# No meeting of the engines between gates and mixing, nor between attention and up projections, with single waits in its place

## Chip, cores and metric

The kernel runs on one core of a Trainium2 chip. TensorE (PE) multiplies, VectorE (DVE), ScalarE (ACT) and GpSimd (POOL) do the rest, SyncE (SP) starts the loads of weights, POOL those of most other tensors. The engines run side by side and order themselves by semaphores alone. The metric is the time of one execution on the device in microseconds (us), given as the median of several runs.

## What is computed

Two transformer blocks on 512 positions, width 2048. The change touches the first one only, where the input projection, three attentions, a gated sum of three up projections and an output projection follow each other:

```python
(a_q, a_ckv, i_q, i_k, i_w, a_gate, b_q, b_k, b_v, b_gate,
 c_q, c_gate, mix_gate) = split_cols(h @ w_in[l], IN_SIZES)
...
oa = dsa_attention(qa, ka, va, iq, ik, iw, bias_a, topk) * jax.nn.silu(a_gate)
...
ob = sliding_window_attention(qb, kb, vb, sinks_b[l], bias_b) * jax.nn.silu(b_gate)
...
oc = memory_attention(qc, kc, vc) * jax.nn.silu(c_gate)
g_a, g_b, g_c = jnp.split(jax.nn.sigmoid(mix_gate + gate_bias[l]), N_BRANCH, axis=-1)
merged = g_a * (oa @ w_up_a[l]) + g_b * (ob @ w_up_b[l]) + g_c * (oc @ w_up_c[l])
x = x + merged @ w_o[l]
```

`dsa_attention` picks each query's keys by an indexer: `score = sum over 16 heads of iw * relu(iq @ ik)`, then the 128 highest.

## The kernel before

**Chunks and groups.** All weights are cut into chunks of 128 x 2048 numbers (1 MB). A projection group `g` yields 256 columns for 512 positions from two chunks, 2g and 2g+1, of 48 products each. A product of full precision is three matmuls (`mm3`, L391 to L393), since every chunk is split into a rounded part and the rest: ACT writes `w_hi` (`split_hi`, L375) and DVE `w_lo` (`split_lo`, L380). There are two buffers each of `w_raw`, `w_hi` and `w_lo`, even chunks in the first, odd ones in the second. PE may not start a chunk before both parts are there (`chunk_ready`), and ACT may not overwrite `w_hi` before PE is done with the chunk two before (`chunk_used`). A chunk's 48 matmuls are 8 row tiles x 2 column halves x 3. SP loads `w_raw` as soon as DVE is through with it.

**Stages.** First come the query groups and 8 gate groups (`G_GATE`), whose two halves lie in PSUM banks 0, 1 or 2, 3 in turn; ACT takes Tanh (L1266), DVE multiplies (L1763) and POOL stores to `g_d` (L2249). Then 24 mixing groups from `G_MIX` on fill banks 0 and 1; ACT takes their Tanh (L1285, `mix_out`) and POOL stores them to `mix_d`. In the first 8 of them `idx_units` (L764) puts 12 small indexer matmuls, in banks 2 to 7, ahead of a group's four quarters (`gemm_part`); ACT takes Relu of these (L1298), DVE adds them up. In the other 16, attention items 2 to 17 stand between the quarters: logits in banks 2 and 3, transposed probabilities in 4 and 5, the result in bank 6; DVE writes it out as `o_st` (L1948, semaphore `o_ready`), POOL stores it to `o_d`.

**Up projections.** Eight groups from `G_UP` on (`up_group`). Their moving operand is the attention result: POOL loads `o_d` in six parts of 3, 3, 4, 4, 1 and 1 row tiles into `o_raw` (L2328, `PARTS_1`), ACT rounds each part into `act_b[0]` (L1106, `part_hi`) and DVE writes the rest into `act_b[1]` (L1956, `part_lo`). `act_b` lies where the attention's operands lay. A group holds three sums: row tiles 0 to 5 in banks 0, 1; 6 to 9 in banks 2, 3; 10 to 15 in banks 4, 5. DVE multiplies each with the gates in `mixg` (L1967), which POOL loads from `mix_d` (L2350), and adds them (L1980, L1985).

**Meetings.** Between the gates and the mixing, and again between the attention and the up projections, all four engines call `meet`: each lets its own work end (`drain`), counts up the semaphore `barrier` and waits until all four have done so. For the second meeting POOL counts up early, while its last stores are still to come. Nothing that an engine has behind the meeting starts before the last one arrives.

Of the kernel before, what the change touches and what calls it, by code (L numbers as in the profile page):

```python
# [22 lines left out]
ALU = mybir.AluOpType  # L23
# [103 lines left out]
def build_kernel(nc, wst, xt_in, mem_in, par_in, con_in, pos_in, tab1_in, tab2_in, rpb_in, lng_in, lnb_in, out):  # L127
# [21 lines left out]
    with ctx:  # L149
# [213 lines left out]

        def meet(eng, n):

            eng.drain().then_inc(barrier, 1)
            eng.wait_ge(barrier, 4 * n)

# [190 lines left out]
        def _(pe):  # L559
# [185 lines left out]
            meet(pe, 1)  # L745


# [19 lines left out]
            with pe.Fori(0, 4) as i:  # L767
                for par in range(2):
                    g, t = 2 * i + (G_MIX + par), 2 * i + par
                    for hs in range(4):  # L770
                        if hs == 0:
                            pe.wait_ge(iq_loaded[par], 16 * i + 16)
                            idx_units(t, par)
                            pe.wait_ge(ev_act, g - 1)
                        gemm_part(g, hs, act_a)
# [113 lines left out]

            up_group(0, first=True)  # L890
# [210 lines left out]
        def _(act):  # L1101
# [173 lines left out]
            meet(act, 1)  # L1275
# [62 lines left out]
            for kind, it0, n in (("B", 2, ITEMS_B), ("C", 8, ITEMS_C), ("A", 12, ITEMS_A)):  # L1338
                with act.Fori(0, n // 2) as i:
                    for par in range(2):  # L1340
                        it = 2 * i + (it0 + par)
                        g = 2 * i + (G_MIX + 6 + it0 + par)
                        for hs in range(4):
                            att_act(kind, it, hs)
                            if hs == 0:
                                split_hi(act, 2 * g + 1, 1)
                            elif hs == 2:
                                split_hi(act, 2 * g + 2, 0)
                        mix_out(g, i, par, 6 + it0)
            meet(act, 2)  # L1350

# [6 lines left out]
            for p in range(len(PARTS_1)):  # L1358
                part_hi(PARTS_1, p, 1)
            with act.Fori(0, 8) as j:  # L1360
                g = j + G_UP
                hi2(g)
                act.wait_ge(up_ch, 5 * j + 5)
                copy(act_a[0][:, bass.ds(2 * j, 2), :], m_acc[:], scale=0.5).then_inc(up_hi, 1)

# [121 lines left out]
        def _(dve):  # L1487
# [309 lines left out]
            meet(dve, 1)  # L1797
# [152 lines left out]
            meet(dve, 2)  # L1950
# [8 lines left out]
            for p in range(len(PARTS_1)):  # L1959
                part_lo(PARTS_1, p, 0)  # L1960
            with dve.Fori(0, 8) as j:
                g = j + G_UP

                def gated(c, dst):

                    for n in range(2):
                        last = dve.scalar_tensor_tensor(out=dst[:, n, :], in0=mixg[:, c, n, :], scalar=1.0,  # L1967
                                                        in1=bank[2 * c + n][:], op0=ALU.add, op1=ALU.mult)
                    last.then_inc(up_ev, 1)

                split_lo(dve, 2 * g + 1, 1)
# [18 lines left out]
                                         op0=ALU.mult, op1=ALU.subtract).then_inc(up_lo, 1)  # L1990

# [187 lines left out]
        def _(pool):  # L2179
# [70 lines left out]
            meet(pool, 1)  # L2250
# [57 lines left out]

            def step(n_it, i, par, g, nxt):

                mix_store(g, i, par, n_it)
                pool.wait_ge(o_ready, 2 * i + (n_it - 5 + par))
                pool.nop(nofuse=True)
                pool.dma_start(o_d[2 * i + (n_it - 8 + par)], o_st[par][:]).then_inc(o_out[par], 16)
# [15 lines left out]
            for n_it, count, same, after in ((8, ITEMS_B, next_b, load_c), (14, ITEMS_C, load_c, next_a),  # L2330
# [4 lines left out]
                if not after:  # L2335
                    pool.drain().then_inc(barrier, 1)

                    for s in range(2):
                        pool.wait_ge(o_out[s], 128)
                    for p in range(4):  # L2340
                        load_part(o_d, PARTS_1, p)
                i = count // 2 - 1
                for par in range(2):
                    step(n_it, i, par, 2 * i + (G_MIX + n_it + par), after)
            pool.wait_ge(o_out[0], 144)
            load_part(o_d, PARTS_1, 4)
            pool.wait_ge(barrier, 8)
# [8 lines left out]
            pool.wait_ge(o_out[1], 144)  # L2356
            load_part(o_d, PARTS_1, 5)
# [88 lines left out]
            pool.wait_ge(barrier, 12)  # L2446
# [81 lines left out]
```

## Time and profile before

| | |
|---|---|
| median of 3 runs | 2747.0 us (2746.95 to 2748.36) |
| the profiled execution: its time, its span | 2748.42 us, 2746.9 us |
| PE busy | 2651.1 us, 97% of the span |
| DVE, ACT, POOL busy | 1191.5, 765.5, 249.7 us |
| mean granted TensorE clock | 0.984 of full speed |
| PE on the chain that ended last | 92% |

The span runs from the first to the last instruction of the profiled execution. Times in rows count from its start. "Idle before" is the time in which an engine did nothing ahead of an instruction, with what released it. An engine's time is worth something only where PE waits for it. The granted clock says at what share of 2.4 GHz the matmuls of a stretch ran; 0.50 is the lower level, 1.2 GHz.

### The profile page before, as it was taken

Reading aid. Unit: us, or ns where it says so; the run is one execution under the profiler, and the core shown is the slowest. Engines: PE = TensorE matmul, PEld = TensorE weight load, DVE = VectorE, ACT = ScalarE, POOL = GpSimd, SP = SyncE. Lnnn points to the kernel's source line nnn. Section 1 sums busy time; section 2 is a strip of 40 time slices with the busy share of each in tenths; the row PEclk is TensorE's granted clock in tenths of the full one; section 3 lists DMA queues with packets and bytes.
Section 4 is the critical chain, followed back from the end, with each engine's and each line's share of the span. In section 5 each row is a group of like instructions: output and inputs, shape, how many; then the busy total and the mean of one; then the engine's idle time right before and its main releaser. Section 6 shows DMA issues by size and latency. Waiting matters only on the chain.

```text
span 2746.9 us, 34039 instructions
## 1 busy us (share of the span) xinstructions
PE 2651.1 (97%) x12748; PEld 2132.9 (78%) x12748; DVE 1191.5 (43%) x2113; ACT 765.5 (28%) x1092; POOL 249.7 (9%) x385
## 2 busy tenths in 40 slices
PE   6959999998999999999999999999999999999998
PEld 5758888887777778888788888777777777777787
DVE  4636222222335775545455332444444444434425
ACT  5321221222332332323222222332233223222321
POOL 4111000000000110111000000000001111211000
PEclk8989999999999999999999999999999999999999
DMA  7454433333343443435444444232232222323432
GB/s 219 114 163 153 143 107 115 115 122 110 111 141 114 148 139 123 161 138 194 151 162 159 158 148 135 90 98 94 94 107 87 92 89 93 99 99 105 180 117 93
DMA packets 70545, 348.80 MB, mean 127 GB/s; under 512 B 11699, under 2 KB 11699, under 8 KB 42275
## 3 DMA queue, kind: packets, MB, share of 16 engines
q1 hardware_dynamic: 38148, 241.28, 25.9%
q0 software_dynamic: 32320, 106.46, 12.2%
q8 instruction: 53, 0.87, 0.1%
q14 instruction: 24, 0.20, 0.0%
HBM read 298.74 MB, written 50.45 MB: 127 GB/s over the span
## 4 chain that ended last, share of the span: by engine, by line
PE 92%; DMA 2%; DVE 2%; ACT 1%; issue 1%; POOL 0%; POOLq 0%; SPq 0%; ACTq 0%; DVEq 0%
PE bank L391 25%; PE bank L393 25%; PE bank L392 25%; PE bank L1069 5%; PE bank L955 2%; PE bank L937 2%; PE bank L1093 2%; PE bank L925 1%; DMA w_raw<-wst 1%; DVE w_lo L380 1%; PE bank L824 1%; PE bank L805 1%; PE bank L786 1%; DMA mem_raw<-mem_t 1%; PE bank L764 1%
## 5 line engine op out<-in xcount | busy, mean ns | idle before, releaser
L380 DVE TENSOR_TENSOR w_lo<-w_raw,w_hi 128x2048 fp32r<-128x2048 f32 x211 | 486.9, 2308 | 527.8 <-ACT w_hi L375 527.8
L391 PE MATMUL bank<-act_a,w_hi 128*128 128x512 f32 (+1 forms) x1672 | 660.8, 395 | 5.5 <-ACT stage L1285 4.1
L393 PE MATMUL bank<-act_a,w_hi 128*128 128x512 f32 (+1 forms) x1672 | 652.5, 390 | 0.0
L392 PE MATMUL bank<-act_a,w_lo 128*128 128x512 f32 (+1 forms) x1672 | 651.8, 390 | 0.0
L391 PE MATMUL bank<-act_b,w_hi 128*128 128x512 f32 x1280 | 505.2, 395 | 7.7 <-DVE act_b L1956 5.2
L375 ACT ACTIVATE w_hi<-w_raw 128x2048 fp32r<-128x2048 f32 x210 | 401.0, 1910 | 395.9 <-PE bank L393 316.0
L393 PE MATMUL bank<-act_b,w_hi 128*128 128x512 f32 x1280 | 499.6, 390 | 0.0
L392 PE MATMUL bank<-act_b,w_lo 128*128 128x512 f32 x1280 | 499.2, 390 | 0.0
L391 PEld LDWEIGHTS bank<-act_a,w_hi 128*128 128x128 f32 (+1 forms) x1672 | 314.2, 188 | 79.9 <-issue 16.1
L393 PEld LDWEIGHTS bank<-act_a,w_hi 128*128 128x128 f32 (+1 forms) x1672 | 313.9, 188 | 66.8
L392 PEld LDWEIGHTS bank<-act_a,w_lo 128*128 128x128 f32 (+1 forms) x1672 | 314.5, 188 | 63.3
L391 PEld LDWEIGHTS bank<-act_b,w_hi 128*128 128x128 f32 x1280 | 240.9, 188 | 57.9 <-issue 7.3
L393 PEld LDWEIGHTS bank<-act_b,w_hi 128*128 128x128 f32 x1280 | 240.8, 188 | 50.9
L392 PEld LDWEIGHTS bank<-act_b,w_lo 128*128 128x128 f32 x1280 | 241.1, 188 | 48.3
L1380 ACT ACTIVATE prob<-prob,nmx 128x512 f32<-128x512 f32 (+1 forms) x128 | 77.8, 609 | 346.4 <-DVE nmx L1493 346.4
L1069 PE MATMUL bank<-w_hi,act_b 128*128 128x512 f32 x384 | 119.5, 393 | 0.4 <-ACT act_b L1106 0.4
L1285 ACT ACTIVATE stage<-bank,half_b 128x512 f32<-128x512 f32 x48 | 30.3, 683 | 231.0 <-PE bank L393 231.0
L2017 DVE CUSTOM_DVE_ANT_0 prob<-bank,b 128x512 f32<-128x512 f32 x64 | 41.7, 688 | 104.8 <-PE bank L925 104.7
L1493 DVE TENSOR_SCALAR prob<-prob,rden 128x256 f32<-128x256 f32 (+1 forms) x216 | 83.5, 396 | 6.8
L1069 PEld LDWEIGHTS bank<-w_hi,act_b 128*128 128x128 f32 x384 | 72.3, 189 | 15.6 <-issue 0.7
L1069 PE MATMUL bank<-w_lo,act_b 128*128 128x512 f32 x192 | 75.0, 391 | 0.0
L955 PEld LDWEIGHTS bank<-prob_t,v_tok 128*64 128x64 f32 x768 | 40.9, 137 | 38.6 <-issue 35.8
(286 smaller groups left out, 2205.7 us busy)
## 6 DMA issues: line engine op xcount, KB each, us to landing
w_raw<-wst SPq DMA_DIRECT2D x215, 1024.0 KB, 4.9
mix_d<-stage POOLq DMA_DIRECT2D x24, 512.0 KB, 3.0
mixg<-mix_d POOLq DMA_DIRECT2D x8, 1536.0 KB, 6.8
b<-rows_2d POOLq DMA_DIRECT2D x16, 448.0 KB, 7.4
x_raw<-x_t SPq DMA_DIRECT2D x8, 512.0 KB, 8.2
q_d<-stage POOLq DMA_DIRECT2D x8, 512.0 KB, 3.2
g_d<-stage POOLq DMA_DIRECT2D x8, 512.0 KB, 3.2
qb<-q_d POOLq DMA_DIRECT2D x16, 256.0 KB, 3.9
```

What stands on the lines that cost most here:

```text
L375: act.activation(w_hi[s][:], w_raw[s][:], ACT.Copy).then_inc(hi_ready, 1)
L380: dve.tensor_tensor(w_lo[s][:], w_raw[s][:], w_hi[s][:].bitcast(F32), ALU.subtract).then_inc(lo_ready, 1)
L391: pe.matmul(out_ap, l_hi, r_hi, start=start, stop=False)
L392: pe.matmul(out_ap, l_lo, r_hi, start=False, stop=False)
L393: return pe.matmul(out_ap, l_hi, r_lo, start=False, stop=stop)
L937: last = pe.transpose(bank[T_BANK[e]][:, b * P:(b + 1) * P], prob[:, 2 * (cc % 2) + e, b * P:(b + 1) * P], ident)
L955: last = pe.matmul(bank[O_BANK][64 * e:64 * e + 64, c * P:(c + 1) * P], v_tok[par][:, vb, 64 * e:64 * e + 64], prob_t[e][:, b, :], start=( ...
L1069: last = pe.matmul(bank[4 * s + b][:], act_b[l][:, k, b * P:(b + 1) * P], wt(r[c % 2], kt, 0, 2 * GC, 2 * GC), start=(k == 0 and n == 0 an ...
L1093: last = pe.matmul(dst[:], act_b[l][:, k, b * P:(b + 1) * P], wt(r[c], kt, 0, 2 * GC, 2 * GC), start=False, stop=(k == KT - 1 and n == 2), ...
L1380: act.activation(pr, pr, ACT.Exp, bias=nmx[:, cc, e:e + 1], accum_out=rs[:, cc, e:e + 1]).then_inc(e2_ready, 1)
L1493: return dve.tensor_scalar(dst, src, by, None, ALU.mult)
L2017: ins = dve.tensor_tensor_reduce(out=dst, in0=src[:], in1=b2[2 * par + e][:, 384 - P * tb:896 - P * tb], scale=1.0, scalar=-3.4e38, op0=AL ...
```

## The change

Both meetings and the function `meet` go, and single semaphores take their place.

At the first one PE starts the first mixing group's first quarter (banks 0, 1) as soon as the gate group before the last has been read from these banks, and puts the 12 indexer matmuls behind this quarter, with a wait for the last gate group's DVE read. Elsewhere the indexer stays ahead of the first quarter. Two of the 8 items are now written out ahead of the loop.

At the second one the three sums of an up group are in banks 2, 3 (row tiles 0 to 5), 0, 1 (6 to 9) and 4, 5 (10 to 15), so that the first one does not touch the banks of the last mixing group; PE waits for `o_ready` 18 (the last item's result written), and for ACT's last Tanh only before the second sum. ACT rounds parts 0 and 1 ahead of the last Tanh, and the odd weight chunk ahead of parts 4 and 5; DVE keeps the same order. POOL stores the last item's result and loads parts 4 and 5 ahead of the last store to `mix_d`; the gates' load comes after that store, as before. The drains go too.

```diff
-            meet(pe, 1)
-
+            pe.wait_ge(ev_dve, G_MIX - 2)
...
-            with pe.Fori(0, 4) as i:
+            def idx_group(i, par):
+
+                g, t = 2 * i + (G_MIX + par), 2 * i + par
+                first = isinstance(i, int) and i == 0 and par == 0
+                if first:
+                    pe.wait_ge(ev_act, G_MIX - 2)
+                    gemm_part(g, 0, act_a)
+                    pe.wait_ge(ev_dve, G_MIX - 1)
+                    pe.wait_ge(qcp, 10)
+                pe.wait_ge(iq_loaded[par], 16 * i + 16)
+                idx_units(t, par)
+                pe.wait_ge(ev_act, g - 1)
+                for hs in range(1 if first else 0, 4):
+                    gemm_part(g, hs, act_a)
...
-            meet(pe, 2)
-
-
-            UP = ((0, 6, (0, 1)), (6, 10, (2, 3)), (10, 16, (4, 5)))
+
+
+            UP = ((0, 6, (2, 3)), (6, 10, (0, 1)), (10, 16, (4, 5)))
...
+                            if first and c == 1:
+                                pe.wait_ge(ev_act, G_UP - 1)
...
+            pe.wait_ge(o_ready, 18)
             up_group(0, first=True)
...
-            meet(act, 1)
...
+                if last:
+                    act.wait_ge(o_ready, 18)
+                    for p in range(2):
+                        part_hi(PARTS_1, p, 1)
+                mix_out(g, i, par, 6 + it0)
...
+            for p in range(2, 4):
                 part_hi(PARTS_1, p, 1)
...
+            split_hi(act, 2 * G_UP + 1, 1)
+            for p in range(4, 6):
+                part_hi(PARTS_1, p, 1)
...
+            split_hi(act, 2 * G_UP + 2, 0)
+            up_hi_out(0)
...
-            meet(dve, 2)
...
-            for p in range(len(PARTS_1)):
+            for p in range(4):
                 part_lo(PARTS_1, p, 0)
...
+            split_lo(dve, 2 * G_UP + 1, 1)
+            for p in range(4, 6):
+                part_lo(PARTS_1, p, 0)
...
-            meet(pool, 1)
...
+            step(n_it, i, 0, g, None)
+            o_store(n_it, i, 1)
             pool.wait_ge(o_out[0], 144)
             load_part(o_d, PARTS_1, 4)
-            pool.wait_ge(barrier, 8)
+            pool.wait_ge(o_out[1], 144)
+            load_part(o_d, PARTS_1, 5)
+            mix_store(g + 1, i, 1, n_it)
```

How the order changes is seen at two places. PE where the gates end and the mixing begins, before (lines of the kernel before; `qb_92` is the indexer's operand):

```order
L393 MATMUL bank<-act_a_56,w_hi_52 128x512
L742 REGISTER_ALU
L742 COMPARE_AND_BRANCH
L767 UNCONDITIONAL_BRANCH [waits barrier]
L767 ISA
L759 ISA [waits iq_loaded0]
L764 MATMUL bank<-ik_t,qb_92 128x512 [waits idx_relu]
```

and the same place in the changed kernel, first the loop's end, then (21 matmuls of the quarter left out) the quarter's end:

```order
L736 COMPARE_AND_BRANCH
L385 MATMUL bank<-act_a_55,w_hi_51 128x512 [waits hi_ready,lo_ready,ev_act,ev_dve]
L386 MATMUL bank<-act_a_55,w_lo_53 128x512
L387 MATMUL bank<-act_a_56,w_hi_51 128x512
```

```order
L387 MATMUL bank<-act_a_56,w_hi_51 128x512
L758 MATMUL bank<-ik_t,qb_92 128x512 [waits iq_loaded0,idx_relu,q_ssq_copied,ev_dve]
L758 MATMUL bank<-ik_t,qb_92 128x512
L758 MATMUL bank<-ik_t,qb_92 128x384 x2
L758 MATMUL bank<-ik_t,qb_92 128x256 x2
L385 MATMUL bank<-act_a_55,w_hi_51 128x512 [waits ev_act]
```

A quarter of 24 matmuls now stands where the wait for the barrier stood. ACT between the last attention item and the up groups, before (`stage_133` is the last Tanh, `act_b_57` a rounded part):

```order
L375 ACTIVATE w_hi_51<-w_raw_49 128x2048 [waits chunk_used]
L1285 ISA [waits staged_out1,chunk_used]
L1285 ACTIVATE stage_133<-bank,half_b 128x512
L1285 ISA
L1285 ACTIVATE stage_133<-bank,half_b 128x512
L1339 REGISTER_ALU
L1339 COMPARE_AND_BRANCH
L1106 ACTIVATE act_b_57<-o_raw 128x1536 [waits o_loaded0,barrier]
L1106 ACTIVATE act_b_57<-o_raw 128x1536 [waits o_loaded1]
L1106 ACTIVATE act_b_57<-o_raw 128x2048 [waits o_loaded2]
L1106 ACTIVATE act_b_57<-o_raw 128x2048 [waits o_loaded3]
```

and in the changed kernel:

```order
L369 ACTIVATE w_hi_51<-w_raw_49 128x2048 [waits chunk_used,w_loaded0]
L1113 ACTIVATE act_b_57<-o_raw 128x1536 [waits o_loaded0,o_ready]
L1113 ACTIVATE act_b_57<-o_raw 128x1536 [waits o_loaded1]
L1291 ACTIVATE stage_133<-bank,half_b 128x512 [waits staged_out1,chunk_used]
L1291 ACTIVATE stage_133<-bank,half_b 128x512
L1113 ACTIVATE act_b_57<-o_raw 128x2048 [waits o_loaded2]
L1113 ACTIVATE act_b_57<-o_raw 128x2048 [waits o_loaded3]
L369 ACTIVATE w_hi_52<-w_raw_50 128x2048 [waits chunk_used,w_loaded1]
L1113 ACTIVATE act_b_57<-o_raw 128x512 [waits o_loaded4]
L1113 ACTIVATE act_b_57<-o_raw 128x512 [waits o_loaded5]
```

Parts 0 and 1 moved ahead of the last Tanh, the odd weight chunk ahead of parts 4 and 5.

## Rows read from the trace of the kernel before

**Rows 1.** The waits of PE, whole run: us in total, times, longest.

```profile
PE bank L764 <- POOLq L366: 8.2, 1, 8.2
...
PE bank L391 <- DVE act_b L1956: 5.2, 1, 5.2
```

**Rows 2.** Timeline at the first meeting: start, duration, engine, what, idle before.

```profile
654.35 0.39 PE L393 MATMUL bank<-act_a,w_hi 128*128 128x512 f32 x1
...
657.39 0.72 POOL L2249 DMA_DIRECT2D g_d<-stage  x1 [20.93 <-DVE stage L1763]
...
662.97 4.21 PE L764 MATMUL bank<-ik_t,qb 64*128 64x512 f32 x12 [8.23 <-POOLq L366]
...
665.13 1.28 ACT L1298 ACT_TABLE_LOAD   x1 [2.16 <-PE bank L764]
...
666.43 1.26 ACT L1298 ACTIVATE prob<-bank 128x512 f32<-128x512 f32 x3
...
669.52 2.29 DVE L380 TENSOR_TENSOR w_lo<-w_raw,w_hi 128x2048 fp32r<-128x2048 f32 x1 [0.55 <-ACT w_hi L375]
```

**Rows 3.** The chain that ended last, second and third indexer units: start, duration.

```profile
689.19 2.14 PE bank L764 x12
713.31 2.14 PE bank L764 x12
```

**Rows 4.** Busy time by stretch: us, PE, PEld, DVE, ACT, POOL, granted clock, DMA.

```profile
663.00:667.20 4.20, 4.20 (x13) 1.95 (x13) 0.00 (x0) 2.06 (x3) 0.00 (x0) 0.51 0.00 0
```

**Rows 5.** Timeline at the second meeting, PE.

```profile
1325.69 0.77 PE L391 MATMUL bank<-act_b,w_hi 128*128 128x512 f32 x1 [5.18 <-DVE act_b L1956]
...
1339.86 0.47 PE L391 MATMUL bank<-act_b,w_hi 128*128 128x512 f32 x1 [1.32 <-DVE w_lo L380]
```

**Rows 6.** Timeline at the second meeting, DVE and ACT.

```profile
1315.05 0.69 DVE L1948 SCALAR_TENSOR_TENSOR o_st<-bank,gb 128x512 f32<-128x512 f32 x1 [1.74 <-PE bank L824]
...
1352.53 1.23 DVE L1985 TENSOR_TENSOR m_acc<-m_acc,m_tmp 128x1024 f32<-128x1024 f32 x1
...
1374.29 1.23 DVE L1985 TENSOR_TENSOR m_acc<-m_acc,m_tmp 128x1024 f32<-128x1024 f32 x1
...
1320.65 1.26 ACT L1285 ACTIVATE stage<-bank,half_b 128x512 f32<-128x512 f32 x2 [9.66 <-PE bank L393]
...
1334.95 0.63 ACT L1106 ACTIVATE act_b<-o_raw 128x512 fp32r<-128x512 f32 x1 [5.89 <-DMA o_raw<-o_d]
```

**Rows 7.** Timeline of POOL before and at the second meeting.

```profile
1280.77 3.05 POOL L2328 DMA_DIRECT2D o_raw<-o_d  x4 [7.10 <-issue]
...
1326.05 0.76 POOL L2350 DMA_DIRECT2D mixg<-mix_d  x1 [1.98 <-DMA mix_d<-stage]
```

**Rows 8.** Busy time by stretch, behind the second meeting; columns as in rows 4.

```profile
1325.70:1328.00 2.30, 2.30 (x6) 1.82 (x7) 2.30 (x2) 2.30 (x2) 1.31 (x2) 0.50 0.61 166
```

**Rows 9.** Groups by shape, 1315 to 1340: count, busy us, mean ns, idle before.

```profile
L1956 DVE TENSOR_TENSOR act_b<-o_raw,act_b 128x2048 fp32r<-128x2048 f32 x2 | 4.5, 2284 | 0.0
L1956 DVE TENSOR_TENSOR act_b<-o_raw,act_b 128x1536 fp32r<-128x1536 f32 x2 | 3.4, 1754 | 7.9 <-ACT act_b L1106 7.9
...
L1106 ACT ACTIVATE act_b<-o_raw 128x2048 fp32r<-128x2048 f32 x2 | 3.7, 1894 | 0.0
L1106 ACT ACTIVATE act_b<-o_raw 128x1536 fp32r<-128x1536 f32 x2 | 2.9, 1474 | 0.2 <-ACTq L366 0.2
```

**Rows 10.** DMA issues, 1230 to 1330: count, size, us from issue to landing.

```profile
o_raw<-o_d POOLq DMA_DIRECT2D x2, 1024.0 KB, 11.6
...
mixg<-mix_d POOLq DMA_DIRECT2D x1, 1536.0 KB, 8.3
```

**Rows 11.** Timeline of PE at the first attention item.

```profile
876.80 0.66 PE L819 MATMUL bank<-prob_t,vb 128*64 128x128 f32 x8 [1.68 <-DVE prob_t L1887]
```

**Rows 12.** Busy time by stretch, other places; columns as in rows 4.

```profile
880.00:882.00 2.00, 2.00 (x6) 1.56 (x5) 0.29 (x1) 1.68 (x1) 0.00 (x0) 0.50 0.00 0
...
1700.00:2200.00 500.00, 499.59 (x2680) 390.71 (x2682) 215.94 (x444) 146.62 (x232) 27.77 (x44) 1.00 0.29 95
```

More of the change, by code:

```diff
@@ L765, in idx_units @@
                                   ik_t[half, 0:P * (tb + 1)], start=True, stop=True).then_inc(i_psum, 1)
-            with pe.Fori(0, 4) as i:
-                for par in range(2):
[L769 to L775, printed above, removed]
+            def idx_group(i, par):
[11 more added lines that the diff above has]
+                    gemm_part(g, hs, act_a)
+            for par in range(2):
+                idx_group(0, par)
+            with pe.Fori(1, 4) as i:
+                for par in range(2):
+                    idx_group(i, par)
             def qk(kind, it, k, q, kk):
@@ L1336, in att_act @@
                     turned_act(kind, it, 3)
[L1338 to L1350, printed above, removed]
             def part_hi(parts, p, loads):
@@ L1957, in part_lo, with up_out @@
                                   ALU.subtract).then_inc(olo_s, 1)
-            for p in range(len(PARTS_1)):
+            for p in range(4):
                 part_lo(PARTS_1, p, 0)
-            with dve.Fori(0, 8) as j:
+            split_lo(dve, 2 * G_UP + 1, 1)
+            for p in range(4, 6):
+                part_lo(PARTS_1, p, 0)
+            def up_out(j):
                 g = j + G_UP
@@ L1967, in gated @@
                         last = dve.scalar_tensor_tensor(out=dst[:, n, :], in0=mixg[:, c, n, :], scalar=1.0,
-                                                        in1=bank[2 * c + n][:], op0=ALU.add, op1=ALU.mult)
+                                                        in1=bank[(2, 0, 4)[c] + n][:], op0=ALU.add, op1=ALU.mult)
                     last.then_inc(up_ev, 1)
-                split_lo(dve, 2 * g + 1, 1)
+                if not (isinstance(j, int) and j == 0):
+                    split_lo(dve, 2 * g + 1, 1)
                 dve.wait_ge(mg_loaded, 16 * j + 16)
@@ L1990, in _ @@
                                          op0=ALU.mult, op1=ALU.subtract).then_inc(up_lo, 1)
+            up_out(0)
+            with dve.Fori(1, 8) as j:
+                up_out(j)
             with dve.Fori(0, 4) as i:
@@ L2307, in _, with o_store @@
                                    channel_multiplier=1).then_inc(cz_s, 1)
-            def step(n_it, i, par, g, nxt):
-                mix_store(g, i, par, n_it)
+            def o_store(n_it, i, par):
                 pool.wait_ge(o_ready, 2 * i + (n_it - 5 + par))
@@ L2314, in step @@
                 pool.dma_start(o_d[2 * i + (n_it - 8 + par)], o_st[par][:]).then_inc(o_out[par], 16)
+            def step(n_it, i, par, g, nxt):
+                mix_store(g, i, par, n_it)
+                o_store(n_it, i, par)
                 if nxt:
@@ L2334, in _ @@
                         step(n_it, i, par, 2 * i + (G_MIX + n_it + par), same)
[L2335 to L2341, printed above, removed]
-                i = count // 2 - 1
-                for par in range(2):
-                    step(n_it, i, par, 2 * i + (G_MIX + n_it + par), after)
+                i = count // 2 - 1
+                g = 2 * i + (G_MIX + n_it)
+                if after:
+                    for par in range(2):
+                        step(n_it, i, par, g + par, after)
+            for s in range(2):
+                pool.wait_ge(o_out[s], 128)
+            for p in range(4):
+                load_part(o_d, PARTS_1, p)
+            step(n_it, i, 0, g, None)
+            o_store(n_it, i, 1)
             pool.wait_ge(o_out[0], 144)
             load_part(o_d, PARTS_1, 4)
-            pool.wait_ge(barrier, 8)
+            pool.wait_ge(o_out[1], 144)
+            load_part(o_d, PARTS_1, 5)
+            mix_store(g + 1, i, 1, n_it)
             def load_gates(j):
@@ L2445, in _ @@
                 pool.wait_ge(y_out[s], 128)
-            pool.wait_ge(barrier, 12)
+            pool.wait_ge(barrier, 4)
             def load_x1(n_out, s):
```

28 lines of the change are left out of this document (19 added, 9 removed).

## The prediction, made before the changed kernel ran

> **What bounds the kernel now.** I read the waits of PE first. PE is busy for 97% of the span, so what counts is where it stands still or runs slowly. Of its waits in the middle of the run two are long, 8.2 us at the indexer's first matmul and 5.2 us at the first up projection [rows 1], and these are the two meetings. The timelines around them come next, and the granted clock beside them, since a stall of PE can be paid twice: once idle, once in matmuls at the lower level.
>
> First meeting. The last gate matmul starts at 654.35. ACT and DVE finish the gates, POOL issues its store at 657.39 and then drains, and the next PE work, the 12 indexer matmuls, starts at 662.97 after 8.23 us of idle time whose releaser is POOL's queue [rows 2]. These 12 take 4.21 us where later items take 2.14 [rows 2, 3], and the clock of this stretch is 0.51, the lower level, after the idle time [rows 4]. The meeting so costs 8.23 + (4.21 - 2.14) = 10.30 us.
>
> Second meeting. PE is idle for 5.18 us until 1325.69, waiting for the first split part of the attention result; then the first chunk of 48 matmuls runs, then PE idles 1.32 us more for the `w_lo` of the odd chunk [rows 5]. A matmul at full clock takes 0.227 us: two up groups lie 1374.29 - 1352.53 = 21.76 us apart [rows 6], for 96 matmuls. The chunk took 1339.86 - 1.32 - 1325.69 = 12.85 us against 48 x 0.227 = 10.88, so 1.97 us went to the clock, which was at 0.50 at its start [rows 8]. Sum: 5.18 + 1.97 + 1.32 = 8.47 us.
>
> Together 18.8 us, the most that the change can win at its two places.
>
> **The first place, step by step.** PE goes on at 654.35 + 0.23 = 654.58 with a quarter of 24 matmuls. Its weights were split while the last gate group ran, and its banks 0, 1 held the gate group before the last, which was read a whole group earlier, so neither wait can hold it. The quarter ends at 654.58 + 24 x 0.227 = 660.0 and the indexer starts at about 660.1. It waits for DVE's read of banks 2, 3, which was over before POOL's store at 657.39 [rows 2]: 2.7 us to spare. No idle time, so the clock should stay at its upper level.
>
> What is late next is the odd chunk's `w_lo`, because only one quarter (5.4 us) now stands between the indexer and the chunk, where two (10.9 us) stood. PE wants the chunk at 660.1 + 2.1 + 5.4, with some 0.1 for starting up again, at 667.8. ACT first loads a table, does 3 Relus and then splits. From the table load to the end of `w_lo` it is 669.52 + 2.29 - 665.13 = 6.68 us, and the table load came 2.16 us after the indexer's start, at the lower clock [rows 2]. At the upper clock I take half of this, 1.1, and at most 1.4. So `w_lo` ends at 660.1 + 1.1 + 6.7 = 667.9, at most 668.2, and one engine sees another's end about 0.14 later, as ACT's last Tanh at 1320.65 does PE's end at 1325.69 - 5.18 = 1320.51 [rows 5, 6]: a new wait of 0.2 to 0.5 us, of which I take 0.3. Below it stands nothing if the engines overlap better. Gain here: 10.3 - 0.3 = 10.0 us.
>
> One rule of the Trainium skill speaks against this. The table load lasts 1.28 us and the first Relu starts 1.30 after it [rows 2]. "ScalarE: Activation LUTs", section "What ACT_TABLE_LOAD costs", has every switch at about 2.66 us, load and drain together; by that the new wait would be an estimated 1.4 us longer and the gain here 8.6. The row has no such drain behind the load, and I go by the row.
>
> The POOL drain that was the meeting's last arrival leaves the path: POOL still waits for its stores, but nothing of its queue is wanted before the second item, 24 us later [rows 3].
>
> **The second place.** The last mixing matmul leaves PE free at 1325.69 - 5.18 = 1320.51. Then PE wants, in turn:
> - The last item's result. DVE has written it at 1315.05 + 0.69 = 1315.74 [rows 6], 4.8 us early.
> - Part 0 of `act_b`. The loads of parts 0 to 3 are issued at 1280.77 [rows 7] and land within 11.6 us of their issue [rows 10], 20 us early. ACT copies part 0 in 1.47 us and DVE subtracts in 1.75 [rows 9]: 1315.74 + 1.47 + 1.75 and two hand-overs of 0.14 gives 1319.2. PE does not wait, 1.3 us to spare. Part 1 ends 1.75 later, at 1320.9, and is wanted after 18 matmuls, at 1324.6.
> - The last Tanh, for banks 0, 1. ACT has part 1 behind it at 1318.8, so Tanh runs as before at 1320.65 for 1.26 us [rows 6]; wanted at 1320.51 + 36 x 0.227 = 1328.7.
> - Parts 2 and 3 and the odd chunk. ACT: 1321.9 + 1.89 + 1.89 [rows 9] = 1325.7, then the split of the weights, 1.9, to 1327.6. DVE, in the same order, starts at 1323.8 and does 2.28, 2.28 and 2.29 [rows 2, 9]: 1330.7. PE wants the chunk at 1320.51 + 10.88 = 1331.4. This is the tightest step, 0.7 us to spare; between 0 and 1 us of wait lies within what these rows allow, and I take 0.
> - Parts 4 and 5. Before, part 5 landed just ahead of 1334.95, after a wait of 5.89 us on ACT [rows 6], with the weights queued behind. Now both loads are issued some 5 us earlier and the odd chunk is ahead of them; wanted at 1320.51 + 84 x 0.227 = 1339.6.
> - The gates. Their load stays behind the last store, at about 1326.05 [rows 7], and lands 8.3 later [rows 10], at 1334.4. It holds up DVE, with the split of the next group's even chunk queued behind the first product: two products of 1.3 us in all, then 2.29, ends at 1338.1, wanted at 1320.51 + 21.76 = 1342.3. Covered by 4 us.
>
> So all of the 8.5 us goes. The swap of the banks costs nothing, as it is the same number of reads and matmuls.
>
> **Does the gain stay?** Behind the second meeting PE is busy for 499.59 of 500 us at clock 1.00 in a long stretch [rows 12]. A stage bound by PE passes on an earlier start in full, and no engine or load there keeps a time of its own.
>
> **Sum.** 10.3 - 0.3 + 8.5 = 18.5 us. The profiled execution took 2748.42 us with a span of 2746.9; the plain runs have 2747.0 as median, so I take the gain from this: 2747.0 - 18.5 = 2728.5 us, with a span of 2728.4.
>
> **The rivals.**
> 1. The new small wait lengthens. A wait of 1.68 us at the first attention item [rows 11] was followed by matmuls at 0.50 [rows 12], some 4 us of them, which costs 2 us more; the wait of 1.32 us at the second meeting was followed by none. If the wait at the first item comes to 1.7 us, as the skill's figure for the table load would have it, it may draw such a stretch behind it: 1.4 + 2.0, giving 2730 to 2733. Against it: the row's 1.30 us. Chance 0.11.
> 2. That half-clock stretch at the first attention item may not come again when all is shifted in time, since its idle time is only a little longer than one that drew none. That gives 2.0 us more: 2726 to 2727. Chance 0.07.
> 3. The second meeting's wait is only moved. If DVE's order makes the odd chunk's `w_lo` or part 0 late by 2 us or more, with the clock falling after it, half of the 8.5 is lost: 2732 to 2737. Against it: the spare times above. Chance 0.05.
> 4. The change does not take effect, a further wait holding PE where the meetings did, POOL's store before all: 2742 to 2752. Neither place's list of waits names such a semaphore. Chance 0.02.
> 5. Slower. Two items, a group and other loop bodies are now written out, hundreds of instructions that PE and the others run once instead of in a loop. If their code came too late, PE would stand still and fall to the lower clock. To end above 2752.5 it would have to lose 24 us: 16 us idle and 16 us of matmuls at half speed. Against it: PE runs the whole start of the kernel from such code, and the waits [rows 1] have none of that size without a releaser. Chance 0.02.
>
> **How the numbers follow.** The forecast, 2727.5 to 2730.5, has 0.73. The range takes in rivals 1 and 2, the end of each unknown (wait at the first item 0 to 2 us, odd chunk 0 to 1 us) and the 1.4 us by which the three runs differ: 2725.5 to 2733. What is left out is rival 3's larger part, 4 and 5, less than 0.1, and a residue for what I have missed. About 0.2%, 5.5 us, is what a measurement can tell from no change. Faster by more than that: all but rivals 4 and 5, 0.95. Within it 0.03, slower 0.02.
>
> **What would show it.** In the changed kernel's trace: the wait for POOL's queue gone from PE's list; the quarter's first matmul 0.23 us behind the last gate matmul; the indexer at 2.1 us, clock 1.00; a wait of PE for `w_lo` of 0.2 to 0.5 us some 13 us after the gates' end. At the second place no idle time of PE between the last mixing and the first up matmul, no clock below 1.00, and no wait 10.9 us later. I am wrong if the sum of PE's waits and slow stretches at the two places is above 3 us, or if the later stages lengthen.

## The result, and the profile after

The changed kernel's median is 2730.75 us (2730.39 to 2733.11, 4 runs) against 2747.68 us of the kernel before beside it; the ratio is 0.9938, 95% interval 0.9925 to 0.9951. A second comparison (below) gave 2729.58 against 2747.58. The prediction was 2728.5 us, range 2725.5 to 2733.0, faster; the first median lies inside this range but 0.25 us above its inner band of 2727.5 to 2730.5, the second one inside both. The profiled execution took 2733.11 us with a span of 2731.5; the kernel before had 2748.42 and 2746.9.

Both long waits of PE are gone from its list. What is left of it behind the gates (waits of PE, 600 us to the end, changed kernel: us in total, times, longest; rows of 0.8 us and less are left out but for the last):

```profile
PE bank L385 <- ACT stage L1291: 3.9, 6, 0.9
PE bank L962 <- DVE prob_t L2073: 2.4, 2, 1.2
PE bank L824 <- DVE prob_t L1908: 1.7, 1, 1.7
PE bank L962 <- ACT prob_t L1113: 1.7, 2, 0.8
...
PE bank L385 <- DVE w_lo L374: 0.2, 1, 0.2
```

**First place.** The timeline of the changed kernel, which answers to [rows 2]; this trace's gates end 3.0 us later than those of before, so its times are 3.0 us on. PE, then ACT, DVE, POOL:

```profile
663.14 2.21 PE L758 MATMUL bank<-ik_t,qb 64*128 64x512 f32 x12
671.19 0.47 PE L385 MATMUL bank<-act_a,w_hi 128*128 128x512 f32 x1 [0.17 <-DVE w_lo L374]
...
657.81 0.60 ACT L1273 ACTIVATE th_g<-bank 128x512 f32<-128x512 f32 x1 [8.96 <-PE bank L387]
...
664.36 1.28 ACT L1304 ACT_TABLE_LOAD   x1 [3.84 <-PE bank L758]
665.66 1.26 ACT L1304 ACTIVATE prob<-bank 128x512 f32<-128x512 f32 x3
...
682.56 1.26 ACT L1291 ACTIVATE stage<-bank,half_b 128x512 f32<-128x512 f32 x2 [9.59 <-PE bank L387]
...
658.44 1.28 DVE L1785 SCALAR_TENSOR_TENSOR stage<-th_g,bank 128x512 f32<-128x512 f32 x2 [7.27 <-ACT th_g L1273]
...
668.75 2.29 DVE L374 TENSOR_TENSOR w_lo<-w_raw,w_hi 128x2048 fp32r<-128x2048 f32 x1 [0.56 <-ACT w_hi L369]
...
660.42 0.72 POOL L2278 DMA_DIRECT2D g_d<-stage  x1 [20.93 <-DVE stage L1785]
```

The indexer (12 matmuls in the trace, of 6 in the program) has no idle time ahead of it and takes 2.21 us instead of 4.21. The only wait is the new one for the odd chunk, 0.17 us. The clock of the stretches (columns as in rows 4) is 1.00 where [rows 4] had 0.51:

```profile
657.60:663.10 5.50, 5.50 (x25) 4.32 (x23) 1.28 (x2) 2.68 (x4) 0.72 (x1) 1.00 0.25 95
663.10:665.30 2.20, 2.20 (x14) 1.10 (x13) 0.00 (x0) 0.94 (x1) 0.00 (x0) 1.00 0.00 0
```

**Second place.** The timeline of the changed kernel's PE shows no idle time between the last mixing matmul and the first up matmul, and none 10.9 us later. The first two rows are PE's, then come ACT's, DVE's and POOL's; they answer to [rows 5 to 7]:

```profile
1313.29 0.39 PE L387 MATMUL bank<-act_a,w_hi 128*128 128x512 f32 x1
1313.52 0.39 PE L385 MATMUL bank<-act_b,w_hi 128*128 128x512 f32 x1
...
1308.95 2.87 ACT L1113 ACTIVATE act_b<-o_raw 128x1536 fp32r<-128x1536 f32 x2 [4.80 <-DVE o_st L1969]
1313.72 1.27 ACT L1291 ACTIVATE stage<-bank,half_b 128x512 f32<-128x512 f32 x2 [1.90 <-PE bank L387]
1314.87 3.72 ACT L1113 ACTIVATE act_b<-o_raw 128x2048 fp32r<-128x2048 f32 x2
...
1310.47 3.43 DVE L1976 TENSOR_TENSOR act_b<-o_raw,act_b 128x1536 fp32r<-128x1536 f32 x2 [1.55 <-ACT act_b L1113]
1316.82 4.49 DVE L1976 TENSOR_TENSOR act_b<-o_raw,act_b 128x2048 fp32r<-128x2048 f32 x2 [2.92 <-ACT act_b L1113]
1321.23 2.29 DVE L374 TENSOR_TENSOR w_lo<-w_raw,w_hi 128x2048 fp32r<-128x2048 f32 x1
...
1325.71 1.29 DVE L1991 SCALAR_TENSOR_TENSOR m_acc<-mixg,bank 128x512 f32<-128x512 f32 x2 [0.99 <-DMA mixg<-mix_d]
...
1336.94 1.23 DVE L2010 TENSOR_TENSOR m_acc<-m_acc,m_tmp 128x1024 f32<-128x1024 f32 x1
...
1319.02 0.75 POOL L2385 DMA_DIRECT2D mixg<-mix_d  x1 [2.91 <-DMA mix_d<-stage]
```

PE's first up matmul follows 0.23 us behind the last mixing matmul, while ACT's last Tanh, which reads banks 0 and 1, has yet to start: the first up sum goes to banks 2 and 3. The clock is 1.00 throughout, where [rows 8] had 0.50:

```profile
1312.00:1324.00 12.00, 12.00 (x55) 9.93 (x54) 9.08 (x6) 7.71 (x7) 1.84 (x3) 1.00 0.49 175
```

**How I compare traces from here.** The kernel's start, up to the end of the gates, varies from run to run, so I count from marks within it, each the start of one instruction: the last gate's Tanh (657.81 here, 654.78 before), the first mixing group's Tanh (682.56), the last mixing group's Tanh (1313.72), the first up group's last sum (1336.94), the end. The stretch between the first two holds the first meeting, that between the third and the fourth the second one.

| us | before | changed | gain |
|---|---|---|---|
| start to last gate's Tanh | 654.78 | 657.81 | -3.03 |
| to the first mixing Tanh (first meeting) | 34.63 | 24.75 | 9.88 |
| to the last mixing Tanh | 631.24 | 631.16 | 0.08 |
| to the first up group's last sum (second meeting) | 31.88 | 23.22 | 8.66 |
| to the end | 1394.37 | 1394.56 | -0.19 |
| from the last gate's Tanh to the end | 2092.12 | 2073.69 | 18.43 |

The gains predicted were 10.0 and 8.5 us, together 18.5.

### The profile page after: what moved, and what is told of

Its sections match the earlier page's. It is cut to its first block, busy times and chain, and to the rows that moved or that the text cites. A ratio compares the mean times of both kernels' runs of the same rounds, so it can differ in the third digit from the quotient of the medians.

```text
span 2731.5 us, 33988 instructions
## 1 busy us (share of the span) xinstructions
PE 2646.4 (97%) x12748; PEld 2129.3 (78%) x12748; DVE 1191.1 (44%) x2113; ACT 765.2 (28%) x1092; POOL 249.5 (9%) x385
## 3 DMA queue, kind: packets, MB, share of 16 engines
q0 software_dynamic: 32320, 106.46, 12.2%
## 4 chain that ended last, share of the span: by engine, by line
PE 93%; DMA 2%; DVE 2%; ACT 2%; issue 1%; POOL 0%; SPq 0%; DVEq 0%; ACTq 0%; POOLq 0%
PE bank L385 25%; PE bank L387 25%; PE bank L386 25%; PE bank L1076 5%; PE bank L944 2%; PE bank L962 2%; PE bank L1100 2%; PE bank L932 1%; DMA w_raw<-wst 1%; DVE w_lo L374 1%; DMA mem_raw<-mem_t 1%; PE bank L829 1%; ACT w_hi L369 1%; PE bank L810 1%; PE bank L935 1%
## 5 line engine op out<-in xcount | busy, mean ns | idle before, releaser
L1291 ACT ACTIVATE stage<-bank,half_b 128x512 f32<-128x512 f32 x48 | 30.4, 683 | 223.1 <-PE bank L387 223.1
```

## Experiments

**Theory**: each meeting cost what PE stood idle at it and what the clock lost behind it, both stretches are now covered by the new order, and PE, the bound, hands the gain on in full. **Rivals**: the two gains overlap or are taken back; the meeting's own hand-overs (the drains, the exchange) were the cost and the new order adds nothing; the changed kernel has a longer start.

### Each place alone

The kernel before with only the first meeting gone:

```diff
-            meet(pe, 1)
+            pe.wait_ge(ev_dve, G_MIX - 2)
...
-            meet(act, 1)
-            meet(dve, 1)
-            meet(pool, 1)
```

(with `idx_group` as in the change, and the counts of the remaining meeting lowered by 4.)

> The kernel before with the first meeting alone removed (the first mixing group's first quarter goes ahead of the indexer); the second meeting stays. Measured from the start of the last gate matmul to the end of the span, which leaves the start of the kernel out, the kernel before takes 2746.9 - 654.35 = 2092.5 us and the changed one 18.4 us less. Theory (the two places are independent and each gives what its idle time and slow clock cost): 10.0 us less than before, 9.5 to 10.5; the indexer at 2.1 us and the upper clock, 0.2 us of wait for w_lo; at the second place the idle times 5.2 and 1.3 us and the clock of 0.50 as before. Rival (the first place's gain is taken back later by work that now comes too early): below 8 us, with a new wait of PE between 690 and 1320 us.

The changed kernel with the first meeting back, in the same way:

> The changed kernel with the first meeting put back, so that only the second one is gone. Theory: from the last gate matmul to the end 8.5 us less than the kernel before, 8.0 to 9.0; at the first place 8.2 us idle and the indexer at 4.2 us as before, at the second no idle time and clock 1.00. With the other run the two gains add up to 18.4 us. Rival (the gains overlap, or one needs the other): the sum misses 18.4 us by more than 1 us.

Measured, in the marks above:

| us | first stretch | second stretch | Tanh to end | median |
|---|---|---|---|---|
| before | 34.63 | 31.88 | 2092.12 | 2748.45 (14 runs) |
| first gone | 24.73 | 31.70 | 2083.67 | 2741.25 (8 runs) |
| second gone | 34.62 | 23.22 | 2081.41 | 2739.91 (6 runs) |
| both gone | 24.75 | 23.22 | 2073.69 | 2730.75 (4 runs, the first comparison) |

The two stretches gave 9.90 and 8.66 us alone, 18.56 in sum; together they gave 18.54. The gains are independent. The sums up to the end missed their ranges, 8.45 instead of 9.5 to 10.5 and 10.71 instead of 8.0 to 9.0, and not at the places: with the first gone the stages behind the first up group ran 1.3 us longer than before, and with the second gone the first attention item ran 1.6 us shorter, because its half-clock stretch did not come (see the section on the hardware). The 1.3 us lie at one place that the change does not touch, the end of the last attention of the second block. PE has several short idle times there in every trace, the longest 1.2 to 1.3 us, and behind them the matmuls run at the lower level for a time that differs from trace to trace. In each of the three traces shown, the window begins within 0.6 us of the first matmul behind these idle times; the first is of the run with the indexer ahead (below), the second of the kernel before, the third of the kernel with the first meeting gone:

```profile
2541.00:2545.00 4.00, 4.00 (x19) 3.31 (x18) 4.00 (x3) 4.00 (x3) 0.00 (x0) 1.00 0.01 4
```

```profile
2552.00:2556.00 4.00, 3.63 (x13) 2.83 (x12) 3.81 (x6) 4.00 (x4) 0.00 (x0) 0.66 0.01 4
```

```profile
2545.00:2549.00 4.00, 3.92 (x9) 3.15 (x10) 4.00 (x6) 4.00 (x3) 0.00 (x0) 0.50 0.00 0
```

From the first up group's last sum to the end these three took 1392.79, 1394.37 and 1395.64 us. Numbers as small as these are read from the stretch, not from the whole.

With the first meeting alone gone, the second place took as long as before (31.70 us against 31.88) but did not split as expected. PE was idle for 5.5 us, and no wait for the odd chunk's `w_lo` followed where 1.3 us were expected; the matmuls in between ran at the lower level for some 6 us where the kernel before had 3.6. The first row is of this run, the second, which tells why the parts are not fixed, of the kernel before:

```profile
1318.70 0.76 PE L391 MATMUL bank<-act_b,w_hi 128*128 128x512 f32 x1 [5.48 <-DVE act_b L1965]
```

```profile
1337.42 2.29 DVE L380 TENSOR_TENSOR w_lo<-w_raw,w_hi 128x2048 fp32r<-128x2048 f32 x1 [1.11 <-ACT w_hi L375]
```

PE could not start the odd chunk before this `w_lo` ended at 1339.71, and what made it late was the landing of part 5 on ACT [rows 6], not PE's clock. At the upper level PE would have waited an estimated 1.97 + 1.32 = 3.3 us for it. So the slow matmuls ahead of this wait added nothing: PE, free at 1320.51, could have started the chunk 10.88 us later, at 1331.39, and started it at 1339.86, which is the whole 8.47 us.

### The order at the first place

The changed kernel with the indexer ahead of the first quarter again, behind one wait for DVE's read:

```diff
                 if first:
                     pe.wait_ge(ev_act, G_MIX - 2)
-                    gemm_part(g, 0, act_a)
                     pe.wait_ge(ev_dve, G_MIX - 1)
...
-                for hs in range(1 if first else 0, 4):
+                for hs in range(4):
```

> The changed kernel, but the indexer stands ahead of the first quarter in the first mixing group too, behind a single wait for the last gate group's DVE read. Theory (the quarter in front is what covers the read): PE idles from its last gate matmul to the end of that read, 656.69 - 654.58 = 2.1 us in the times of the kernel before, and some 0.15 for the hand-over: 2.2 us; the wait for w_lo of 0.2 us goes. Without a fall of the clock the time is 2.0 us longer than the changed kernel's; a wait of 1.7 us elsewhere was followed by some 4 us of half clock, so with a fall 4 to 5 us longer. Rival (dropping the meeting and its drain is all, the order costs nothing): within 0.5 us of the changed kernel.

The timeline of this kernel's PE and the stretches around it (PE, PEld, DVE, ACT, POOL, clock, DMA):

```profile
660.37 3.83 PE L758 MATMUL bank<-ik_t,qb 64*128 64x512 f32 x12 [2.16 <-DVE stage L1784]
...
660.00:662.00 2.00, 1.63 (x6) 0.93 (x8) 0.16 (x1) 0.94 (x2) 0.72 (x1) 0.70 0.00 0
662.00:664.00 2.00, 2.00 (x10) 1.00 (x6) 0.00 (x0) 1.89 (x3) 0.00 (x0) 0.50 0.69 262
664.00:666.00 2.00, 2.00 (x10) 1.56 (x9) 1.68 (x3) 2.00 (x3) 0.57 (x1) 0.95 0.00 0
```

PE idles 2.16 us (2.2 expected) and the indexer runs at the lower clock behind it, 3.83 us instead of 2.21. The stretch is 28.18 us, 3.43 more than in the changed kernel: 2.16 idle and 1.62 for the clock, less the 0.17 of the wait for `w_lo`, which went, make 3.6. That is less than the 4 to 5 us expected with a fall of the clock, since the matmuls at the lower level were over within the indexer. So dropping the meeting alone brings 6.45 of the 9.88 us, and the quarter in front the other 3.43. The rival (the order costs nothing) falls. The median was 2734.05 us (4 runs), 3.3 above the changed kernel's 2730.75.

Two quarters in front instead of one:

```diff
                     gemm_part(g, 0, act_a)
+                    gemm_part(g, 1, act_a)
                     pe.wait_ge(ev_dve, G_MIX - 1)
...
-                for hs in range(1 if first else 0, 4):
+                for hs in range(2 if first else 0, 4):
```

> The changed kernel, but two quarters instead of one stand ahead of the indexer in the first mixing group, so that nothing stands between the indexer and the odd chunk. Theory (the new wait for the odd chunk's w_lo is the time from the indexer's start to this w_lo, 8.05 us in the changed kernel's trace, less what PE has to do in between, 7.9 us with one quarter and 2.3 us with none): a wait of 5.7 us, and up to 2 us lost to the clock behind it; from the last gate's Tanh to the next item's 30.3 to 32.3 us where the changed kernel has 24.75. Rival (the w_lo does not hang on the indexer's Relus): the wait stays at 0.2 us or goes.

Its timeline and the stretches behind the wait:

```profile
671.98 0.77 PE L385 MATMUL bank<-act_a,w_hi 128*128 128x512 f32 x1 [5.83 <-DVE w_lo L374]
...
670.00:674.00 4.00, 2.02 (x5) 1.68 (x6) 4.00 (x5) 2.45 (x3) 0.00 (x0) 0.50 0.24 51
674.00:676.00 2.00, 2.00 (x7) 1.57 (x6) 1.62 (x1) 0.00 (x0) 0.00 (x0) 0.53 0.95 397
```

The wait is 5.83 us (5.7 expected) and the stretch 32.01 us (30.3 to 32.3 expected). This is one run, as are the next ones with the banks as before, the odd chunk behind and POOL's drain left out; they are read by their traces alone. The one quarter between indexer and odd chunk is what hides the Relus and the splits, and one quarter in front is the best of none, one and two.

### The order at the second place

Parts 0 and 1 rounded behind the last Tanh:

```diff
+                mix_out(g, i, par, 6 + it0)
                 if last:
                     act.wait_ge(o_ready, 18)
                     for p in range(2):
                         part_hi(PARTS_1, p, 1)
-                mix_out(g, i, par, 6 + it0)
```

> The changed kernel, but ACT rounds parts 0 and 1 behind the last Tanh instead of ahead of it; no meeting anywhere. Theory (at the second place the work queued behind the meeting is the cost, not the meeting): PE waits for Tanh 1.4, part 0's copy 1.5, its subtraction 1.75 and hand-overs, about 5.0 us, then some 2 us are lost to the clock, and no wait for the odd chunk: 7 us longer than the changed kernel, 6 to 8. Rival (the meeting's own hand-overs made the 5.2 us): less than 2 us longer than the changed kernel.

```profile
1313.28 0.58 PE L385 MATMUL bank<-act_b,w_hi 128*128 128x512 f32 x1 [4.75 <-DVE act_b L1976]
...
1313.00:1316.00 3.00, 2.72 (x7) 2.17 (x8) 3.00 (x2) 3.00 (x2) 0.75 (x1) 0.58 0.37 37
```

PE waits 4.75 us for part 0 with no meeting at this place, and the clock falls behind it. The second stretch is 29.85 us, 6.63 more than in the changed kernel (6 to 8 expected); its median is 2737.16 us (5 runs). Of the 8.66 us at this place, dropping the meeting and the early split of the odd chunk so bring 2.03, and the two copies ahead of Tanh 6.63. Most of what the meeting cost here was so the order that it kept, with these copies behind Tanh.

The banks of the up sums as before, with PE's wait for the last Tanh ahead of the first sum:

```diff
-            UP = ((0, 6, (2, 3)), (6, 10, (0, 1)), (10, 16, (4, 5)))
+            UP = ((0, 6, (0, 1)), (6, 10, (2, 3)), (10, 16, (4, 5)))
...
-                            if first and c == 1:
+                            if first and c == 0:
...
```

> The changed kernel with the banks of the up sums as before (first sum in banks 0, 1), so PE waits for ACT's last Tanh ahead of the first sum. Theory (the swap covers Tanh's 1.26 us and a hand-over): PE idles 1.5 us between the last mixing and the first up matmul, the stretch from the last Tanh to the end of the first up group's sums grows from 23.2 us to 24.7, and to 26.7 if the clock falls behind it, which it did not after 1.3 us of idle time but did after 1.7. Rival (Tanh is done before PE gets there): 23.2 us.

```profile
1313.77 0.47 PE L385 MATMUL bank<-act_b,w_hi 128*128 128x512 f32 x1 [1.45 <-ACT stage L1291]
```

1.45 us idle (1.5 expected), a stretch of 24.94 us (24.7), and no fall of the clock: with the copies ahead of Tanh, the swap is worth 1.7 us. With the copies behind Tanh PE waits for part 0 longer than for Tanh, so the 6.63 us above and these 1.7 are not two parts of a sum; both taken back together were not run.

The odd chunk split behind parts 4 and 5, on ACT and DVE:

```diff
-            split_hi(act, 2 * G_UP + 1, 1)
             for p in range(4, 6):
                 part_hi(PARTS_1, p, 1)
+            split_hi(act, 2 * G_UP + 1, 1)
...
```

> The changed kernel, but ACT and DVE split the odd weight chunk of the first up group behind parts 4 and 5 of the attention result, as before. Theory (parts 4 and 5 now land early, so the chunk is put off by their two subtractions only, 1.29 us, less the 0.9 us it had to spare): PE waits 0.4 us for w_lo, the stretch from the last Tanh to the first up group's sums grows from 23.22 us to 23.6. Rival (the landing of part 5 still holds ACT, as in the kernel before): a wait of 2 us or more.

```profile
1322.78 0.47 PE L385 MATMUL bank<-act_b,w_hi 128*128 128x512 f32 x1 [0.31 <-DVE w_lo L374]
```

0.31 us of wait and a stretch of 23.82 us, 0.60 more. The theory's 0.4 holds; the rival, that part 5's landing still holds ACT, falls. In the kernel before it had held ACT for 5.89 us [rows 6]. There POOL issued its load behind the 1536 KB of the gates' load, 6.3 us after PE's last mixing matmul had ended (1320.51); here, as in the changed kernel, it goes ahead of the last store to `mix_d`, 0.9 us before PE's first up matmul in the changed kernel's trace (1313.52). The first row is of the kernel before, the second of the changed one:

```profile
1326.80 0.55 POOL L2328 DMA_DIRECT2D o_raw<-o_d  x1
```

```profile
1312.59 0.54 POOL L2359 DMA_DIRECT2D o_raw<-o_d  x1 [1.81 <-DMA o_d<-o_st]
```

Which of the two, the earlier issue or the gates' load no longer ahead of it, freed ACT was not tried apart.

### The drain

The kernel before with both meetings, where POOL alone counts up at the first one without draining:

```diff
-            meet(pool, 1)
+            pool.sem_inc(barrier, 1)
+            pool.wait_ge(barrier, 4)
```

> The kernel before with both meetings, but POOL does not drain ahead of counting up at the first one. Theory (POOL's drain behind its last store was the last to arrive, 5.2 us on the chain): PE resumes at about 0.9 us after POOL has issued the store, the idle time falls from 8.2 to 3.8 us, the clock has fallen by then (it was 0.50 from 658 us on, 3.3 us after PE stopped), so the indexer still takes about 4.2 us, and the stretch from the last gate's Tanh to the next item's falls from 34.6 us to 30.2. Rival (all four engines' exchange is what takes the time): above 33 us.

Timeline of PE and POOL, then two stretches with the clock:

```profile
659.64 4.21 PE L764 MATMUL bank<-ik_t,qb 64*128 64x512 f32 x12 [3.10 <-POOLq L2250]
...
659.18 0.72 POOL L2249 DMA_DIRECT2D g_d<-stage  x1 [20.93 <-DVE stage L1763]
...
660.00:662.00 2.00, 2.00 (x6) 0.83 (x6) 0.00 (x0) 0.20 (x1) 0.00 (x0) 0.50 0.68 262
...
664.00:666.00 2.00, 2.00 (x6) 1.57 (x7) 1.64 (x3) 2.00 (x3) 0.57 (x1) 0.54 0.12 18
```

The idle time falls from 8.23 us [rows 2] to 3.10 (3.8 expected), so POOL's drain behind a store just issued was 5.13 us of the meeting. The stretch falls by 4.18 only, from 34.63 to 30.45 us (30.2 expected), as the clock takes one more back: after the long idle time the matmuls ran at the lower level for 4.2 us from the indexer's start, here for 6.2.

### The start of the kernel

> The changed kernel once more, beside the kernel before, since the first comparison gave 16.9 us from four runs each while the two traces, counted from the last gate's Tanh, differ by 18.4. Theory (the start of the kernel, up to the gates' end, varies by some us from run to run and is the same in both): the last gate's Tanh starts anywhere between 652 and 659 us, the rest from there takes 2073.7 us, within 2, and the medians of more runs differ by 17 to 20 us. Rival (the changed program has a longer start): the difference of the medians stays below 17 us.

The median was 2729.58 us (2728.03 to 2732.89, 5 runs) against 2747.58 (9 runs), ratio 0.9938, interval 0.9925 to 0.9952: 18.0 us. The last gate's Tanh started at 654.23 us, the rest took 2072.27 us. Over all traces here this Tanh starts between 652.55 us (parts behind Tanh) and 658.25 us (indexer ahead), with no order by kernel: before 654.78, changed 657.81 and 654.23. So the rival of a longer start falls as far as these traces go; nine runs of the changed kernel have a median of 2730.5 us and 28 of the kernel before 2748.1, which is 17.6 us. I estimate its uncertainty at about one, from the spread of these runs (5.1 us from lowest to highest for the nine); the interval of the second comparison alone is wider, 13 to 21 us. The 28 hold one run on another chip, at 2743.55 us; without it the difference is 17.7.

### One more wait made narrower

DVE waited for POOL's causal fill of the scores ahead of the first attention item, though only the picks read it. In the changed kernel:

```diff
-                    dve.wait_ge(cz_s, 3)
                     dve.sem_inc(topk_s, 1)
...
                                 if kind == "B":
+                                    if par == 0:
+                                        dve.wait_ge(cz_s, 3)
                                     pick(1, 24 * i + (12 * par + 1))
```

> The changed kernel with one more wait made narrower: DVE waits for POOL's causal fill of the scores right before the first pick of the highest scores, which reads them, and no longer ahead of the first attention item's softmax. Theory: DVE starts that softmax some 3 us earlier, PE's waits of 0.5, 1.7 and 0.2 us there go, and the 4 us of half clock behind them (2.0 us lost) with them: the stretch between the Tanh of the last indexer group and that of the first attention group falls from 34.8 us to about 30.4, and the time is 4.4 us shorter than the changed kernel's. Rival (another work of DVE or ACT is late there too): less than 2 us of gain, with a wait of PE for something else.

The first softmax of DVE, in this kernel and, in the second fence, in the changed one:

```profile
849.01 0.88 DVE L1858 SCALAR_TENSOR_TENSOR prob<-bank,rq,bb 128x256 f32<-128x256 f32 x2 [7.26 <-PE bank L791]
```

```profile
855.26 0.88 DVE L1858 SCALAR_TENSOR_TENSOR prob<-bank,rq,bb 128x256 f32<-128x256 f32 x2 [9.78 <-POOL score L2334]
```

Counted from the last gate's Tanh it starts 2.5 us earlier and waits for PE's logits now. PE's waits there shrink to 0.2 us, with no half clock behind them, and the item takes 30.69 us instead of 34.81 (30.4 expected), a gain of 4.12; against the changed kernel's second trace, whose item took 33.19, it is 2.50. The median is 2723.77 us (2723.47 to 2729.01, 5 runs) beside 2729.58 of the changed kernel, ratio to the kernel before 0.992, interval 0.9906 to 0.9933. It beats both kernels. Not all of the 5.8 us between the medians is the wait's: in the trace 1.7 us come from the second block's place shown above, where this run had no half-clock stretch.

## Why the prediction was right, step by step

- **What bounds, and that the gain stays.** Right: the stages between the two places changed by 0.08 us and those behind by 0.19. That these numbers are so small is in part luck, since over all traces the stages behind vary from 1392.8 to 1395.8 us with the clock.
- **Cost of the first meeting, 10.3 us, less a new wait of 0.3.** Right. The indexer starts without idle time, and the table load follows its start by 664.36 - 663.14 = 1.22 us (1.1 to 1.4 predicted). From there to the end of `w_lo` it is 6.68 us, the very number of before. The new wait is 0.17 us, just below the 0.2 to 0.5 predicted (0.3 taken). Measured gain 9.88.
- **The table load.** Relu starts 1.30 us behind the load's start again. The Trainium skill, "ScalarE: Activation LUTs", section "What ACT_TABLE_LOAD costs", has 2.66 us for load and drain together. The trace does not agree: the wait that this would have made an estimated 1.7 us is 0.17, and the measurement decides.
- **Second meeting, 8.5 us, all of it.** Right at 8.66 in sum. The term of 1.97 us for the clock was put down to the wrong cause: by my estimate the wait for the odd chunk would have been longer by as much at the upper level (see "Each place alone"). It did no harm here because the new order took both the idle time and this wait away. Part 0 was split at about 1312.2, 1.3 us ahead of PE (1.3 predicted). The odd chunk's `w_lo` ended at 1323.52, wanted at 1313.52 + 10.88 = 1324.40: 0.9 to spare (0.7 predicted). The gates' first product came 12.2 us after PE's start, where the predicted landing gives 13.9; their load, issued at the predicted place, took 6.7 us and not 8.3, and DVE was covered either way.
- **The swap of the banks.** I wrote that it costs nothing; what it is worth, 1.7 us, I had not worked out.
- **The step that was mis-sized** is the last one, from the sum to the median. The sum (18.5) is that of the traces (18.43), but the runs gave 16.9 and then 18.0 us. I took the three runs' spread of 1.4 us for the noise and set the new time by it. The start of the kernel alone varies by 5.7 us among the traces, and the runs of one kernel by up to 6.6 us (eight runs with the first meeting gone), so a median of 3 or 4 runs is good to a microsecond or two. That the range held is partly luck: it was made wide for rivals 1 and 2 and for longer waits, and not for this.
- **Rivals.** The first did not come: the wait was too short. The second, that the half-clock stretch at the first attention item goes, came in one of the changed kernel's two traces, for 1.6 us and not 2.0; a variant of the kernel before, without POOL's drain, lost the stretch as well, so it is not tied to the change. Rivals 3 to 5 did not come.

## What to carry to other kernels

Price a barrier by what the bounding engine does around it: its idle time, the slower clock behind it, and the next wait down the line; slow matmuls ahead of such a wait are paid by the wait and are not added to it. Then ask what work the barrier kept back. At the first place the meeting itself was the larger part, 6.45 of 9.88 us (leaving out POOL's drain alone gave 4.2), and the quarter of matmuls moved past it brought 3.43; at the second place the two copies moved past it brought 6.63 of 8.66 us. The swap of the banks was worth 1.7 us once the copies had moved. When changes are as small as these, compare stretches between fixed instructions within the trace and leave the kernel's start out.

## What the runs showed of the hardware

- A drain of POOL right behind a DMA that it had issued made 5.1 us of PE's idle time, by one trace with it and one without. The single waits did without it.
- Short idle times of PE and the clock. After 1.32 us [rows 5] and 1.45 us no fall was seen, after 2.16 and 3.10 us there was one, but the length of one wait does not settle it. At the first attention item PE had the same three waits (0.5, 1.7 and 0.2 us) in eight traces with an item of 34.8 us and in two with one of 33.2 (the second meeting alone gone, and the kernel without POOL's drain). In the first of these two the clock stays at 1.00 behind the wait of 1.7 us, in the changed kernel it falls:

```profile
876.00:878.00 2.00, 1.40 (x17) 0.98 (x18) 1.86 (x9) 1.22 (x6) 0.00 (x0) 1.00 0.05 21
878.00:880.00 2.00, 2.00 (x13) 1.74 (x14) 0.72 (x2) 1.22 (x3) 0.00 (x0) 1.00 0.00 0
```

```profile
870.00:872.00 2.00, 1.77 (x19) 1.36 (x20) 1.52 (x8) 0.84 (x4) 0.00 (x0) 0.89 0.00 0
872.00:874.00 2.00, 2.00 (x8) 1.78 (x7) 0.69 (x1) 0.98 (x3) 0.00 (x0) 0.50 0.00 0
```

  The changed kernel's second trace has an item of 33.2 us for another reason. There the clock fell already behind the wait of 0.5 us:

```profile
858.58 1.11 PE L810 MATMUL bank<-con,prob 128*128 128x128 f32 x4 [0.53 <-DVE prob L1515]
...
858.00:860.00 2.00, 1.47 (x7) 1.33 (x7) 1.21 (x3) 1.28 (x1) 0.00 (x0) 0.65 0.04 8
860.00:862.00 2.00, 2.00 (x6) 1.56 (x5) 2.00 (x3) 0.00 (x0) 0.00 (x0) 0.50 0.00 0
```

  From these four matmuls to the eight at which PE waits 1.73 us in the first trace it was 7.87 us in this trace and 7.86 in the first. The slow matmuls took up the time in which PE had to wait anyway, the wait is gone from the list, and the clock did not fall again behind it. So here the matmuls at the lower level cost nothing, since a wait followed that they only filled.

  The Trainium skill, "TensorE: Matmul & The Clock Gate", section "What's actually happening", has the number of slow matmuls at a kernel's start vary between runs of one kernel. Here it varies in the middle: at this place between the changed kernel's two traces, and at the end of the second block's attention from trace to trace. Why the clock falls in one run and not in the next was not tried.
- Why the start of the kernel varies by 5.7 us was not tried either. It lies ahead of both places.
